# Two decoder blocks on one core: the memory operand without its root, and one wide matmul for the high and low operand in the first two parts of the input product

## The reference

```python
h  = rms_norm(x, mix_norm_g)              # x * rsqrt(mean(x*x) + eps) * g
p  = h @ w_in                             # 2048 -> 6408 columns, split into the branches' inputs
m  = rms_norm(mem, mem_norm_g)
kv = m @ xa_wkv                           # 2048 -> 1024 columns
x  = x + mixed_branches(p) @ w_out        # an LRU, an mLSTM and an attention branch
x  = x + cross_attention(rms_norm(x, xa_norm_g) @ xa_wq, kv) @ xa_wo
x  = rms_norm(x, final_norm_g)
```

## Time and profile before

| | us |
|---|---|
| median of 3 runs | 1929.22 (1926.1 to 1930.45) |
| the profiled execution | 1928.11 |
| its span, first to last instruction | 1926.3 |
| TensorE busy | 1786.3 (93%) |
| VectorE busy | 1381.1 (72%) |
| ScalarE busy | 808.3 (42%) |
| mean granted clock of TensorE | 0.965 of 2.4 GHz |

### The profile page before, as it was taken

One profiled execution on the slowest core, in us unless ns is written; L12 is line 12 of the kernel. 1 busy time (PEld: TensorE's weight loads), 2 busy tenths in 40 slices (PEclk: granted clock), 3 DMA queues, 4 the chain that ended last, 5 costly groups with the idle time before them and its releaser, 6 DMA issues.

```text
span 1926.3 us, 26091 instructions
## 1 busy us (share of the span) xinstructions
PE 1786.3 (93%) x10209; PEld 1523.4 (79%) x10209; DVE 1381.1 (72%) x2174; ACT 808.3 (42%) x1273; POOL 13.1 (1%) x26
## 2 busy tenths in 40 slices
PE   7999988997888888999999999998889999999987
PEld 6899988987877867877877777776887877777676
DVE  4788759778899787878688768777782566656544
ACT  6544365633435454233333232233452454445343
POOL 1000000000000000000000000000000010000000
PEclk9999999999999979999999999999899999999989
DMA  6588744525666434345455555554341564343343
GB/s 209 184 269 264 237 146 157 185 88 168 200 217 215 158 120 133 110 163 169 139 169 181 177 173 177 185 193 144 110 136 55 157 214 152 112 139 126 110 134 129
DMA packets 169634, 313.13 MB, mean 163 GB/s; under 512 B 15036, under 2 KB 23592, under 8 KB 169512
## 3 DMA queue, kind: packets, MB, share of 16 engines
q1 hardware_dynamic: 162176, 305.70, 49.2%
q10 hardware_dynamic: 6248, 3.62, 0.7%
q0 software_dynamic: 1088, 2.15, 0.4%
HBM read 309.33 MB, written 2.10 MB: 162 GB/s over the span
## 4 chain that ended last, share of the span: by engine, by line
PE 54%; DVE 6%; ACT 3%; issue 1%; DMA 0%; DVEq 0%; ACTq 0%
PE bank L509 14%; PE bank L511 14%; PE bank L510 14%; DVE w_low L319 2%; PE bank L2631 2%; PE bank L2899 2%; PE bank L2900 2%; PE bank L2901 1%; PE bank L2650 1%; PE bank L2630 1%; PE bank L446 1%; ACT w_high L309 1%; PE bank L2641 1%; DVE big L686 1%; DVE big L2474 0%
## 5 line engine op out<-in xcount | busy, mean ns | idle before, releaser
L509 PE MATMUL bank<-operand,w_high 128*128 128x256 f32 (+1 forms) x2448 | 798.8, 326 | 69.8 <-DVE w_low L319 43.0
L511 PE MATMUL bank<-operand,w_low 128*128 128x256 f32 (+1 forms) x2448 | 786.5, 321 | 0.0
L510 PE MATMUL bank<-operand,w_high 128*128 128x256 f32 (+1 forms) x2448 | 786.5, 321 | 0.0
L319 DVE TENSOR_TENSOR w_low<-raw,w_high 128x1024 fp32r<-128x1024 f32 (+4 forms) x416 | 454.2, 1127 | 179.2 <-ACT w_high L309 177.7
L509 PEld LDWEIGHTS bank<-operand,w_high 128*128 128x128 f32 x2448 | 479.0, 196 | 122.8 <-DVE w_low L319 47.7
L309 ACT ACTIVATE w_high<-raw 128x1024 fp32r<-128x1024 f32 (+4 forms) x416 | 394.3, 980 | 426.7 <-PE bank L511 209.0
L510 PEld LDWEIGHTS bank<-operand,w_high 128*128 128x128 f32 x2448 | 479.3, 196 | 31.2 <-issue 0.7
L511 PEld LDWEIGHTS bank<-operand,w_low 128*128 128x128 f32 x2448 | 478.5, 195 | 30.4
L426 DVE SCALAR_TENSOR_TENSOR ada_acc<-ada_raw,silu_c,ada_acc 128x512 f32<-128x512 f32 x660 | 452.2, 745 | 11.3 <-DMA ada_raw<-in_ada_w 7.8
L509 PE MATMUL bank<-operand_small,w_high 128*128 128x512 f32 (+1 forms) x320 | 123.6, 386 | 5.4 <-DVE big L408 3.3
L510 PE MATMUL bank<-operand_small,w_high 128*128 128x512 f32 (+1 forms) x320 | 119.7, 374 | 0.0
(11 more groups left out here) (375 smaller groups left out, 1567.2 us busy)
## 6 DMA issues: line engine op xcount, KB each, us to landing
ada_raw<-in_ada_w SPq DMA_DIRECT2D x192, 512.0 KB, 4.0
raw<-in_w_in SPq DMA_DIRECT2D x96, 512.0 KB, 4.8
raw<-in_pool_w_in SPq DMA_DIRECT2D x64, 512.0 KB, 5.2
raw<-in_mla_w_in SPq DMA_DIRECT2D x48, 512.0 KB, 4.5
raw<-in_w_out SPq DMA_DIRECT2D x32, 512.0 KB, 5.7
raw<-in_pool_w_out SPq DMA_DIRECT2D x32, 512.0 KB, 5.7
raw<-in_mla_w_out SPq DMA_DIRECT2D x32, 512.0 KB, 4.3
raw<-in_xa_wkv SPq DMA_DIRECT2D x16, 512.0 KB, 4.5
```

Of the source, the lines that this page charges most:

```text
L319: ins = nc.vector.tensor_sub(view(LO[:, slot, ks, :], False), view(RAW[:, slot, ks, :], True), view(HI[:, slot, ks, :], False).bitcast(F32))
L509: pe.matmul(out_, hi, x[:, 0, :], start=first, stop=False, skip_group_check=True)
L510: pe.matmul(out_, hi, x[:, 1, :], start=False, stop=False, skip_group_check=True)
L511: return pe.matmul(out_, lo, x[:, 0, :], start=False, stop=last, skip_group_check=True)
```

## The change

1. **Memory.** kv is now of kind `root1`: the operand is memory times gain, without the root; high part by ACT (four copies with a scale for each quarter, from the transposed memory), low part by DVE (one `scalar_tensor_tensor` for each tile). The root is computed later into `RMEM` and multiplied in when DVE moves kv's tiles out of PSUM. The transposed memory is copied to SBUF by DVE instead of ACT (`dve_turn`). The transposes of x come after kv's chunks 0 and 1, the sums of the memory's squares after chunk 2, those of x after chunk 3. SP loads kv's first chunk ahead of x.
2. **win_a and win_b** are of a new kind `sum1`: the high part of the weights is multiplied in one matmul of 512 columns with high and low operand side by side, which fill the two halves of a PSUM bank; the weights' low part adds to the first half. DVE adds the halves as it moves a tile out (`tensor_reduce` over the two). ACT moves nothing out in these products.
3. **Units.** kv's four units go; po gets 36 instead of 32 (three in each fourth chunk). `act_rows(act, 0, 8)` moves from mixo's chunk 7 to behind the high part of xq's first chunk.

The order of every other product is unchanged. The diff, cut:

```diff
+        self.two_sums = kind == "sum1"
...
-    kv = Product("kv", wkv, 4, 2, 4, 1, "copy1", half=1, dest=XAK, banks=5)
-    win_a = Product("win_a", w_in, 4, 6, 4, 1, "copy1", dest=LX)
-    win_b = Product("win_b", w_in, 4, 1, 3, 1, "copy1", dest=LX + 24, col0=6 * GW)
+    kv = Product("kv", wkv, 4, 2, 4, 1, "root1", half=1, dest=XAK, banks=5)
+    win_a = Product("win_a", w_in, 4, 6, 4, 1, "sum1", dest=LX)
+    win_b = Product("win_b", w_in, 4, 1, 3, 1, "sum1", dest=LX + 24, col0=6 * GW)
...
-    ada = {win_a: 1, xo: 1, po: 2}
+    ada = {win_a: 1, xo: 1}
...
-    SPARSE = {kv: {(0, 2): 1, (0, 3): 1, (1, 0): 1, (1, 1): 1},
-              win_c: {divmod(c, 4): n for c, n in ((3, 1), (7, 1), (8, 1), (9, 1), (10, 2), (11, 1), (12, 1), (15, 1),
+    SPARSE = {win_c: {divmod(c, 4): n for c, n in ((3, 1), (7, 1), (8, 1), (9, 1), (10, 2), (11, 1), (12, 1), (15, 1),
...
-              mixo: {(i, j): 2 for i in range(4) for j in range(2)}}
+              mixo: {(i, j): 2 for i in range(4) for j in range(2)},
+              po: {(i, j): 3 if j == 3 else 2 for i in range(4) for j in range(4)}}
...
+                if p.kind == "sum1":
+                    wait_tile(dve, p, i, n)
+                    both = PB[p.bank[i, n]][:, :].rearrange("p (s t) -> p t s", s=2)
+                    nc.vector.tensor_reduce(d, both, AX.X, ALU.add).then_inc(dve_freed, 1)
...
-            pe.matmul(out_, hi, x[:, 0, :], start=first, stop=False, skip_group_check=True)
-            pe.matmul(out_, hi, x[:, 1, :], start=False, stop=False, skip_group_check=True)
+            if p.two_sums:
+                pe.matmul(bank[:, :].rearrange("p (s t) -> p s t", s=2), hi, x, start=first, stop=False, skip_group_check=True)
+            else:
+                pe.matmul(out_, hi, x[:, 0, :], start=first, stop=False, skip_group_check=True)
+                pe.matmul(out_, hi, x[:, 1, :], start=False, stop=False, skip_group_check=True)
             return pe.matmul(out_, lo, x[:, 0, :], start=False, stop=last, skip_group_check=True)
...
         def dve_product(dve, p, former=None):
...
                         dve_low(dve, p, i, j)
+                    if former and i == 0 and j == 0:
+                        dve_evac(dve, former, former.groups - 1)
+                    if p is win_a and i and j == 0:
+                        dve_evac(dve, win_a, i - 1)
                     dve_ada(dve, p, i, j)
...
             for i in range(2):
                 for j in range(4):
                     if i == 0:
                         front_dve.wait(pe, "lm", j)
+                    pe_chunk(pe, kv, i, j)
+                    if i == 0 and j < 2:
+                        for kk in range(4 * j, 4 * j + 4):
+                            pe_turn(pe, 1, kk)
+                    if (i, j) == (0, 2):
+                        sums("m", 7, SQM_F)
+                    if (i, j) == (0, 3):
+                        pe.wait_ge(tr_free, 16)
+                        sums("x", 5, SQX_F)
+                        front_act.wait(pe, "rm")
...
+            memory_high(0)
             act_high(act, kv, 0, 0)
+            memory_high(1)
+            act_high(act, kv, 0, 1)
+            memory_high(2)
+            memory_high(3)
+            for kk in range(4):
                 act_turn(act, 1, kk)
+            squares("m", 0)
+            squares("m", 1)
+            act_high(act, kv, 0, 2)
+            for kk in range(4, 8):
+                act_turn(act, 1, kk)
+            squares("m", 2)
+            squares("m", 3)
+            act_high(act, kv, 0, 3)
+            act.wait_ge(tr_free, 16)
             for q in range(4):
+                squares("x", q)
+            front_pe.wait(act, "m")
+            front_act.inc(s(RMEM, PB[7][:, 0:T], ACT.Sqrt, bias=EPS, scale=1.0 / D), "rm")
...
-            act_product(act, win_b, former=win_a)
+            act_product(act, win_b, last=False)
             act_high(act, win_c, 0, 0)
...
+            memory_low(0)
             dve_low(dve, kv, 0, 0)
+            memory_low(1)
+            dve_low(dve, kv, 0, 1)
+            memory_low(2)
+            memory_low(3)
+            dve_low(dve, kv, 0, 2)
+            dve_low(dve, kv, 0, 3)
             front_act.wait(dve, "rm")
+            st.inc(v.reciprocal(RMEM, RMEM), "rm")
+            dve_low(dve, kv, 1, 0)
+            st.wait(dve, "rm")
+            dve_evac(dve, kv, 0)
...
+            dve_product(dve, win_a, former=kv)
+            dve_product(dve, win_b, former=win_a)
             dve_low(dve, win_c, 0, 0)
+            dve_evac(dve, win_b, 0)
...
             sp_turn(sp, 0, a["mem"][0])
+            sp_chunk(sp, kv, 0, 0)
             sp_turn(sp, 1, a["x"][0])
-            sp_product(sp, kv)
+            for c in range(1, 8):
+                sp_chunk(sp, kv, *divmod(c, 4))
...
-                if c == 7:
-                    act_rows(act, 0, 8)
...
                 if j == 0:
+                    act_rows(act, 0, 8)
                     operand(3)
```

More of the change, by code:

```diff
@@ L404, in dve_evac @@
                     wait_tile(dve, p, i, n)
-                    nc.vector.tensor_tensor(d, PB[p.bank[i, n]][:, 0:T], RST[:, :], ALU.mult).then_inc(dve_freed, 1)
+                    nc.vector.tensor_tensor(d, PB[p.bank[i, n]][:, 0:T], RMEM if p is kv else RST[:, :], ALU.mult).then_inc(dve_freed, 1)
                 elif p.kind == "gate2":
@@ L757, in pe_front, with sums @@
             ins.then_inc(vec_turned, 1)
[L759 to L764, removed]
+            def sums(key, bank, squares):
+                for q in range(4):
+                    front_act.wait(pe, key, q)
+                    for k in range(4):
+                        ins = pe.matmul(PB[bank][:, 0:T], ones[:, :], squares[q][:, k, :],
+                                        start=q == 0 and k == 0, stop=q == 3 and k == 3)
+                front_pe.inc(ins, key)
             setup.wait(pe, "ones")
[L766 to L769, removed]
             front_dve.wait(pe, "pv")
+            pe.wait_ge(tr_free, 8)
             for i in range(2):
@@ L842, in act_front @@
             high(2)
+            act_high(act, kv, 1, 3)
             high(3)
-            act_high(act, kv, 1, 3)
-            act_product(act, win_a, former=kv, last=False)
+            act_product(act, win_a, last=False)
             act.dma_start(LW[:, 0:4], a["lru_wa"][0].rearrange("g i o -> i g o")).then_inc(lw_in, 16)
@@ L860, in dve_front @@
             dve_setup(dve)
+            for kk in range(8):
+                dve_turn(dve, 0, kk)
             dve.wait_ge(vec_turned, 1)
@@ L863, in dve_front, with memory_low @@
             st.wait(dve, "pv")
[L864 to L865 removed]
+            def memory_low(q):
+                front_act.wait(dve, "hm", q)
                 for k in range(4 * q, 4 * q + 4):
[L867 to L878 removed]
@@ L880, in low @@
-            def low(key, q):
-                front_act.wait(dve, "h" + key, q)
-                x, half = (four_of(CT0, q), 1) if key == "m" else (HFX[q % 2], 0)
-                st.inc(v.tensor_sub(operand_of(half, q, 1), x, operand_of(half, q, 0).bitcast(F32)), "l" + key, q)
-            front_act.wait(dve, "rm")
-            st.inc(v.reciprocal(RST[:, :], RST[:, :]), "rm")
-            normed("m", 0)
-            normed("m", 1)
-            low("m", 0)
-            dve_low(dve, kv, 0, 1)
-            low("m", 1)
@@ L891, in dve_front, with normed @@
-            normed("m", 2)
-            normed("m", 3)
-            low("m", 2)
-            dve_low(dve, kv, 0, 2)
-            low("m", 3)
+                    ins = v.scalar_tensor_tensor(XS[:, k, 1, T:2 * T], tile(CT0 + k), V["mem_g"][:, k:k + 1],
+                                                 XS[:, k, 0, T:2 * T].bitcast(F32), ALU.mult, ALU.subtract)
+                st.inc(ins, "lm", q)
+            def normed(q):
+                front_act.wait(dve, "gx", q)
+                st.wait(dve, "rx")
+                st.inc(v.tensor_tensor(HFX[q % 2], HFX[q % 2], four, ALU.mult), "nx", q)
@@ L896, in dve_front @@
+            dve_low(dve, kv, 1, 0)
+            st.wait(dve, "rm")
+            dve_evac(dve, kv, 0)
+            front_act.wait(dve, "rx")
+            st.inc(v.reciprocal(RST[:, :], RST[:, :]), "rx")
+            normed(0)
+            normed(1)
+            dve_low(dve, kv, 1, 1)
+            low(0)
+            low(1)
+            dve_low(dve, kv, 1, 2)
+            normed(2)
+            low(2)
             dve.wait_ge(sc_act, 2)
```

110 lines of the change are left out of this document (34 added, 76 removed).

## The result

The changed kernel takes 1935.88 us (median of 12 runs, 1932.13 to 1938.87), the one before 1928.45 (12 runs, 1926.1 to 1931.27): a ratio of **1.0035, 95% interval [1.0023, 1.0047]**, slower by 0.35%, some 7 us. The prediction was 1930, within 0.2% of before: the whole interval lies beyond those 0.2%.

What follows compares the result with a forecast made beforehand. TensorE, busy 93% of the span, was taken as the bound. Terms -2.7 -5.8 -3.1 -4 +2 +14.3 = +0.7 gave 1928.8 against the profiled 1928.1, so 1930 us beside the median; own range 1926 to 1934, whole range 1918 to 1940.

Steps and rivals of the forecast that it cites:

- The stands: po chunks (1,1) and (3,0): VectorE waits at a unit for the same chunk's slab sums, TensorE behind it; +14.3 us.
- The wide matmul: win_a and win_b: one 512-column matmul for two of 256 saves 13.4 ns in each of 432 blocks; -5.8 us.
- Rival D: win_a and win_b: the fused matmul streams no faster; +5.8, 1936 us; chance 0.05.
- Rival C: win_a: VectorE becomes the bound, the reduction costing 1.15 us; +5.9, 1936 us; chance 0.07.
- The memory's part: Kernel's front: without the memory's root TensorE starts at 19.2 us, win_a near 92 instead of 95.05; -2.7 us.
- Rival A: The front gives more than the walk says, waits halved; faster, 1923 down to 1917 us; chance 0.28.
- The end of the front stage: Ahead of win_c: the next weights' split comes before the evacuation, and three reductions follow TensorE's end; -3.1 us.
- The middle: win_c chunk 22 to mixa: VectorE's wait for the slab vanishes, some returned at mixa's start; -4 us.
- mixo: A slab closes at mixo's last chunk instead of its sixth, delaying the sums ScalarE waits for; +2 us.
- B: po's two waits are the whole story, front and middle together giving less than 8; slower, 1937 us; chance 0.18.

Runs made afterwards that it cites:

- e1: Changed kernel with the memory product's four units in win_b instead of po, so no stands in po; 1923.71 us, ratio 0.9973 to the kernel before.
- e2: Changed kernel with po's 36 units shifted so that each slab closes with a chunk; 1922.75 us, ratio 0.9968 to the kernel before.
- e6: Changed kernel with po's second stand moved one chunk later, (3,0) to (3,1), which put four units in po's last chunk; 1938.82 us, ratio 1.0054 to before.
- e9: Changed kernel with po's first stand moved one chunk earlier, (1,1) to (1,0), with four units in chunk 2; 1942.05 us, ratio 1.0075 to before.
- e7: Changed kernel with the wide matmul written as two of 256 columns, VectorE's reduction kept; 1937.93 us, ratio 1.005 to the kernel before.
- e12: e1 with win_a and win_b as before the change: the memory's part and the units in win_b; 1924.7 us, ratio 0.9984 to the kernel before.
- e10: Kernel before with one line changed: win_c's chunks 22 and 23 take 1 and 2 units, not 2 and 1; 1921.4 us, ratio 0.9968 to before.
- e4: Kernel before with only the wide matmul and VectorE's sums in win_a and win_b; 1921.63 us, ratio 0.9965 to before.
- e5: e1 with win_c's chunks 22 and 23 taking 1 and 2 units, so no stand anywhere; 1915.32 us, ratio 0.993 to the kernel before.
- e8: Changed kernel with the wide matmul reading 512 consecutive columns, not two pieces, so it computes something else; 1934.81 us, ratio 1.0032 to the kernel before.

## Why the prediction was right, and where its sum was not

The sum was +0.7 and the traces have +10.0. The measured 1935.9 lies outside the forecast's own range (1926 to 1934) and inside the whole one (1918 to 1940), which took in the slower cases; "slower" had a chance of 0.33. So the places and the order of size of the terms were right, and the width of the range did the rest. By its steps:

- **The stands**: right in place and size (6.1 and 9.7 us from matmul to matmul, 6.0 and 9.6 predicted), shown by e1, e2, e6 and e9. The term was +14.3 and is +18.0. The two waits are 3.9 and 7.5, as predicted. The clock took 4.6 (the chunks behind the stands take 1.7 and 2.9 longer; 3 predicted), and one more slab (1.9) is exposed in po: before, it lay ahead of po's start and was hidden in the wait there. That one I missed.
- **The wide matmul**: mis-sized, -2.7 for -5.8. I took 0.2266 for it, from a stream of 512-column matmuls; between narrow ones it mostly takes 0.233. The Trainium skill (TensorE: Matmul & The Clock Gate, Back-to-back issue gap) gives N/2.4 plus about 2.5 ns for an isolated matmul at the full clock. Worked out from it, an estimate, only some 1.1 us would be saved and the forecast would have been 1934.7, near the measured 1935.9. It comes out near for another reason, since its constant isn't seen here: two narrow matmuls cost 0.240, one wide 0.227 to 0.233, and the part is worth 2.7 and not 1.1. Rival D (no faster) is wrong by half: with two matmuls of 256 columns the block is 0.360 (e7), with the wide one 0.353. Rival C (VectorE as the bound) is refuted by the 159.00 of 159.00.
- **The memory's part**: the start came at 20.08 (19.2 predicted), and the first chunk took 8.3 us instead of 6.5, at a mean clock of 0.85 over 20 to 40 us; win_a starts 1.1 earlier instead of 2.7. In the eight other traces with the new front it starts 1.4 to 2.8 earlier, so the trace of after shows this term at its smallest. In time e12 gives it 3, with an interval that holds both numbers. Rival A fell.
- **The end of the front stage**: -3.1, exact.
- **The middle**: -5.7 for -4. win_c's stand goes with 5.3 by mixa's start (4.4 of it at chunk 23), and e10 shows that most of this is kept. Another 1.8 come in win_c ahead of the stand, where e4 and e12 gain 1.5 and 2.2 against the same trace of before and e1 only 0.1, so it is no part of the change; and mixa gives back 1.3.
- **mixo**: +5.6 for +2, the largest error beside po's. Most of it is the slab that I had walked, the one at mixo's end: it costs 4.4 and not 2, since TensorE also waits 2.29 for VectorE's last units before it can sum them, a wait that the prediction put at nothing. The slab after chunk 3 I had not walked at all, though the same count of units gives it; it has the same wait (2.45), and here the low clock behind it.

Rivals C and D (1936) have the nearest number and B (the stands are the whole story, the middle gives nothing, 1937) the next, none of them its reason: VectorE never bounds win_a, the wide matmul does stream faster, and the middle gave more than forecast, which mixo and the missing half of part 2 took back. Each term was off by under 4 us, and only the middle and the stretch behind po went the other way; the three large errors, wide matmul (3.1), mixo (3.6) and po (3.7), all had the same sign and are the most of the missing 9.3.

## What to carry to other kernels

When work that is cut into batches is moved, count where every batch closes and opens afterwards, all along the kernel; a batch that opens in the chunk in which the last one closes stops the engine that fills it, and everything behind in its order, for the length of the sums and more. Look at what stands behind the stop, on that engine and on the next two: here TensorE idled 3.9 us or 7.5 behind the same wait. A batch whose last unit the side engine ends later than the main engine its chunk costs more than its sums: in mixo and ahead of xq TensorE first waited 2.5 and 2.3 us for the units. And look for such a stop in the kernel as it is: the one that was there was worth 6.2 us in one line, by the medians twice the memory's part (3), though the intervals overlap.

## What the runs showed of the hardware

- A 512-column matmul between 256-column ones runs at one of two paces, 0.3465 or 0.353 us for the pair, for whole groups at a time in the same code (e2 and e5 show both); the wide read's second piece costs nothing measurable (0.353 with it and without, e8).
- Stops of 3.9 and 7.5 us in po's busy stretch cost 1.7 and 2.9 more in the clock: the first matmuls after them start 0.43 us apart instead of 0.23 (1221.30 to 1221.73 and on in the trace of after; granted clock 0.51 over 1220.7 to 1224.1), the level of 1.2 GHz. The cost doesn't follow the length of the stop: e6's second one, also 3.90, costs 2.7, and e9's last, 7.49, costs 1.75.
- A reduction of two halves, 128x512 of PSUM to 128x256, takes 692 ns, as long as one to 128x1 (690).
